# Index pass of a two-layer sparse-attention decoder: head pairs in one rectifier instruction, decode rows two at a time

## The reference

```python
s = jnp.einsum('bqhe,bke->bqhk', qi, ki).astype(jnp.float32)     # 8 index heads of 64
score = jnp.einsum('bqhk,bqh->bqk', jax.nn.relu(s), wi.astype(jnp.float32))
score = jnp.where(admissible[None], score, -jnp.inf)
_, idx = lax.top_k(score, topk)
```

## Time and profile before

| | us |
|---|---|
| median of 3 runs | 5874.4 (5874.07 to 5880.87) |
| profiled execution, its own time | 5873.04 |
| its span | 5871.3 |
| PE busy / PE weight loads | 5420.4 (92%) / 3003.6 |
| DVE busy | 3496.8 (60%) |
| ACT busy | 1748.2 (30%) |
| POOL busy | 1279.0 (22%) |
| mean granted TensorE clock | 0.913 |

### The profile page before, as it was taken

How to read it: one execution, slowest core, us unless ns; L and a number is a source line. 1 busy time by engine, 2 the same in 40 slices (tenths; PEclk the granted TensorE clock), 3 DMA queues, 4 the chain that set the end, 5 groups by cost and what they waited for, 6 DMA issues and landing times.

```text
span 5871.3 us, 75115 instructions
## 1 busy us (share of the span) xinstructions
PE 5420.4 (92%) x25302; PEld 3003.6 (51%) x25302; DVE 3496.8 (60%) x6149; ACT 1748.2 (30%) x3005; POOL 1279.0 (22%) x1215
## 2 busy tenths in 40 slices
PE   7996899999999998999989868999999999889999
PEld 4441344644555556664454314446445556567643
DVE  2561599999877542223425616999997765412234
ACT  2451100100455652220034511001005566522200
POOL 3210034400112871000032100344001128710000
PEclk9895799999999998878998957999999999987899
DMA  1001211211210023544310012112112200245532
GB/s 59 22 4 35 57 36 30 69 48 63 75 58 32 33 67 125 159 146 136 109 36 22 4 37 59 33 31 69 48 62 73 83 9 32 67 127 171 161 97 93
DMA packets 345087, 392.90 MB, mean 67 GB/s; under 512 B 102839, under 2 KB 266770, under 8 KB 341042
## 3 DMA queue, kind: packets, MB, share of 16 engines
q1 hardware_dynamic: 326322, 384.54, 20.9%
q10 hardware_dynamic: 18432, 4.20, 0.3%
HBM read 298.77 MB, written 89.93 MB: 66 GB/s over the span
## 4 chain that ended last, share of the span: by engine, by line
PE 79%; DVE 8%; ACT 4%; issue 4%; ACTq 2%; DMA 1%; POOL 1%; SPq 1%; DVEq 0%; POOLq 0%
PE banks L780 16%; PE banks L783 12%; PE banks L1724 8%; DVE arena L392 4%; PE banks L302 4%; PE banks L1485 4%; PE banks L1053 4%; PE banks L1085 3%; PE banks L1070 3%; PE banks L1510 3%; PE banks L1268 3%; PE banks L1477 2%; PE banks L1283 2%; PE banks L1258 2%; PE banks L541 2%
## 5 line engine op out<-in xcount | busy, mean ns | idle before, releaser
L882 DVE TENSOR_SCALAR_CACHE_REDUCE arena<-arena 128x384 uint8<-128x384 f32 (+14 forms) x960 | 1404.6, 1533 | 6.5
L780 PE MATMUL banks<-arena 128*128 128x512 f32 x2176 | 937.4, 592 | 0.0
L783 PE MATMUL banks<-arena 128*128 128x384 f32 (+3 forms) x2336 | 725.6, 466 | 18.4 <-SPq L146 18.4
L780 PEld LDWEIGHTS banks<-arena 128*128 128x128 f32 x2176 | 409.9, 189 | 523.2 <-issue 523.2
L1313 POOL TENSOR_SCALAR arena<-arena 128x128 f32<-128x128 f32 (+15 forms) x192 | 577.8, 3021 | 144.0 <-DVE arena L1343 144.0
L1169 DVE TENSOR_TENSOR_SCAN arena<-arena 128x129 f32<-128x129 f32 (+3 forms) x480 | 519.3, 1126 | 144.9 <-ACT arena L1097 122.7
L783 PEld LDWEIGHTS banks<-arena 128*128 128x128 f32 (+1 forms) x2336 | 420.1, 184 | 287.5 <-issue 83.2
L1724 PE MATMUL banks<-arena 128*128 128x512 f32 (+1 forms) x1088 | 473.4, 598 | 14.5 <-SPq L146 14.5
L1332 DVE CUSTOM_DVE_ANT_0 arena<-banks,arena 128x512 f32<-128x512 f32 (+3 forms) x480 | 274.1, 608 | 339.0 <-PE banks L1258 318.3
L328 PE MATMUL banks<-arena 64*128 64x512 f32 (+3 forms) x1216 | 423.0, 607 | 22.9 <-ACT arena L374 17.4
L392 DVE SCALAR_TENSOR_TENSOR arena<-arena 128x512 f32<-128x512 f32 (+3 forms) x532 | 401.3, 754 | 55.9 <-DVE arena L392 0.7
(11 more groups left out here) (194 smaller groups left out, 6640.4 us busy)
## 6 DMA issues: line engine op xcount, KB each, us to landing
arena<-in_cache_sb_kv SPq DMA_DIRECT2D x256, 384.0 KB
arena<-in_cache_dsa_kv SPq DMA_DIRECT2D x256, 128.0 KB
arena<-in_x_prompt SPq DMA_DIRECT2D x32, 512.0 KB, 4.4
arena<-mixT SPq DMA_DIRECT2D x32, 512.0 KB, 4.1
arena<-xs SPq DMA_DIRECT2D x32, 512.0 KB, 4.5
arena<-in_w_in SPq DMA_DIRECT2D x8, 1536.0 KB, 7.2
out<-arena SPq DMA_DIRECT2D x64, 192.0 KB, 1.9
mixT<-arena SPq DMA_DIRECT2D x40, 256.0 KB, 2.2
```

Source lines behind the costliest of these rows:

```text
L780: m = nc.tensor.matmul(bank[i % 4][:, :], W2[c % 2][:, k, j * P:(j + 1) * P], xT[:, k, t * FREE:(t + 1) * FREE], start=(k == 0), stop=(k = ...
L783: m = nc.tensor.matmul(bank[i % 4][0:rows_of(t), 0:WD[name]], xT[:, k, t * P:t * P + rows_of(t)], W2[c % 2][:, k, 0:WD[name]], start=(k == ...
L882: nc.vector.tensor_scalar(out[0:r, 0:v.shape[-1]], v, thr[0:r, t:t + 1], 0.0, ALU.is_ge, ALU.add, accum_out=cnt[0:r, t:t + 1]).then_inc(s_ ...
```

## The change

In the index pass a unit is now a pair of heads (t, c, h), h = 0 to 3: two matmuls into two neighbouring banks, one rectifier over both (2 x w columns), two VectorE operations. There are two pair buffers instead of four single ones. The 584 index columns are computed in two halves of 292 for each of the eight slices k, instead of 512 and then 72.

In the decode index pass a unit is a pair of sequences. Their keys stand side by side in 128 columns, so that one transpose serves both; two matmuls on the two halves of the array give 128 rows of products; one matmul with a 128 x 16 `xsel` sums them to 16 rows, which VectorE copies straight to rows 32g to 32g+15 of `scs`. The store to `SCD` and the read back are gone. The hardware loop is written out. VectorE makes two of the five key copies. Three key buffers rotate. The 32 page loads of the first pair are issued by SP in the index pass, at its iteration t = 12; of the other 96, SP issues 64 and ScalarE 32, the latter behind the rectifiers of pairs 0 and 1. `scs` has 128 rows with gaps that are zeroed, so in the stick-breaking stage its store to `SBD` is eight DMAs instead of one. The selection and bias steps work on 128 rows of it instead of 64. `hsel` is made by 16 instead of 8 instructions at the start.

```diff
@@ start_gpsimd
-            v = hsel[:]
-            for h in range(HIDX):
...
+            for e in range(2):
+                v = hsel[:].rearrange("p (q e) -> p q e", e=2)[:, :, e]
+                for h in range(HIDX):
+                    nc.gpsimd.affine_select(out=v, in_=v, compare_op=ALU.not_equal, fill=1.0, base=-e * NS - h * NQ,
...
@@ index pass
-        ir = [carve(FREE) for _ in range(4)]
+        ir = [carve(2 * FREE).rearrange("p (e k) -> p e k", e=2) for _ in range(2)]
...
+                if t == NT - 4:
+                    for e in range(2):
+                        sample_keys_load(sp, l, 0, e)
             for r in range(3):
                 sp.wait_ge(s_ks[r], at(s_ks[r], 16 * (l + 1) * (KSTORES[r] + (KS_EXTRA if r == NT % 3 else 0))))
+            sample_index_queries(sp, l, 0)
...
                     for k in range(KC):
-                        nc.tensor.matmul(bank[0][0:rows_of(s), :], xT[:, k, s * P:s * P + rows_of(s)], W1[:, k, 0:FREE],
-                                         start=(k == 0), stop=(k == KC - 1))
-                    for k in range(KC):
-                        m = nc.tensor.matmul(bank[1][0:rows_of(s), 0:72], xT[:, k, s * P:s * P + rows_of(s)], W1[:, k, FREE:584],
-                                             start=(k == 0), stop=(k == KC - 1))
+                        for v in range(2):
+                            m = nc.tensor.matmul(bank[v][0:rows_of(s), 0:HALFW], xT[:, k, s * P:s * P + rows_of(s)],
+                                                 W1[:, k, v * HALFW:(v + 1) * HALFW], start=(k == 0), stop=(k == KC - 1))
...
-                        for h in range(HIDX):
-                            a = h % 2 * HD
-                            pe.wait_ge(s_ir, at(s_ir, l * NIU + i - 3))
...
+                        for h in range(HIDX // 2):
+                            pe.wait_ge(s_ir, at(s_ir, l * NIU + i - 1))
+                            for e in range(2):
+                                a = e * HD
+                                k = nc.tensor.matmul(bank[4 + 2 * (i % 2) + e][:, 0:w], iqT[t % 2][a:a + HD, h, :], ikT[a:a + HD, c * FREE:c * FREE + w],
+                                                     start=True, stop=True)
+                            k.then_inc(s_iz, 1)
...
-                            act.wait_ge(s_ie, at(s_ie, l * NIU + i - 3))
-                            nc.scalar.activation(ir[b][:, 0:w], bank[4 + b][:, 0:w], ACT.Relu).then_inc(s_ir, 1)
+                            act.wait_ge(s_ie, at(s_ie, 2 * (l * NIU + i - 1)))
+                            nc.scalar.activation(ir[b][:, :, 0:w], z[:, :, 0:w], ACT.Relu).then_inc(s_ir, 1)
...
@@ decode index pass
+        def sample_keys_load(queue, l, g, e):
+            for j in range(NPG):
+                b = 2 * g + e
+                pg = queue.value_load(pages[0:1, b * NPG + j:b * NPG + j + 1], min_val=0, max_val=N_POOL - 1)
+                queue.dma_start(xk[g % 3][:, j, e * HD:(e + 1) * HD], dsa_kidx[l, ds(pg, 1), :, :].rearrange("o p d -> (o p) d")).then_inc(s_xk[g], 16)
...
+            sp.wait_ge(s_xm0, at(s_xm0, 4 * l + 3))
+            new_rows(0)
+            sample_index_queries(sp, l, 1)
+            sample_keys_load(sp, l, 1, 0)
+            sample_keys_load(sp, l, 1, 1)
+            new_rows(1)
+            sample_index_queries(sp, l, 2)
+            sample_keys_load(sp, l, 2, 0)
+            new_rows(2)
...
+            sample_index_queries(sp, l, 3)
+            sample_keys_load(sp, l, 3, 0)
+            new_rows(3)
             load_chunk(sp, l, 0)
...
+            for g in range(NPR):
...
+                pe.wait_ge(s_xk[g], at(s_xk[g], 16 * 34 * (l + 1)))
+                transposes(g, 0)
                 for c in range(NX + 1):
+                    if c + 1 < NX:
+                        transposes(g, c + 1)
                     if c < NX:
...
+                        scores_of(g, c)
+                    if c >= 1:
+                        summed(g, c - 1)
...
+                keys(g, 0)
+                relu(g, 0)
+                keys(g, 2)
+                relu(g, 1)
+                relu(g, 2)
+                keys(g, 4)
+                relu(g, 3)
+                relu(g, 4)
+                if g < 2:
+                    for v in range(2):
+                        act.wait_ge(s_xtf[v], at(s_xtf[v], XU[v] * (n + 1 - g)))
+                    sample_keys_load(act, l, g + 2, 1)
```

More of the change, by code:

```diff
@@ L241, in build @@
         XUSE = (9, 8)
+        HALFW = 292
         KSTORES = [6, 5, 5]
@@ L1014, in stick_sync @@
             sp.wait_ge(s_bias, at(s_bias, l * NSEL + 1))
-            sp.dma_start(SBD[:, :], scs[0:NS, :]).then_inc(s_bs, 16)
+            for b in range(NB):
+                a = 32 * (b // 2) + b % 2
+                sp.dma_start(SBD[b * NQ:(b + 1) * NQ, :], scs[a:a + 2 * NQ - 1:2, :]).then_inc(s_bs, 16)
             load_stick_qk(sp, l, 1)
```

262 lines of the change are left out of this document (117 added, 145 removed).

## The result

The changed kernel takes 5641.8 us in the median of four runs (5636.9 to 5646.1), the kernel before, run in turn with it, 5877.6 us (5874.1 to 5889.2). The ratio is 0.9595, with an interval of 0.9579 to 0.9612: 4.0% faster, where 3.4% was forecast. The profiled execution took 5646.05 us, the slowest of the four; against its sum of 5672.3 that is 26.3 us less, and the terms behind the difference don't all have one sign.

A forecast was written before the change was run, and what follows sets the result against it. The decode index pass was taken as bound by serial copies, issues and half-clock work, not by a full engine. 5873.0 - 217.2 + 4 + 10 + 2.5 = 5672.3 us; forecast's own range 5650 to 5695, 8-in-10 range 5640 to 5715.

The forecast's parts named there:

- What bounds: Decode index pass: no engine fills it; each sequence is a series of copies, eight issues, rectifier, products, sums at half clock.
- The decode index pass: This stage falls to 106 us in each layer, from 212.3 and 216.9, saving 217.2 us in all.
- cheaper issues: Decode index pass: issues cheaper when written out, or pair 2 waits less; 8 us per stage, 5656 us; chance 0.08.
- the rival of half clock throughout: Decode index pass stays at half clock; both stages end at 128 us, total 5716 us; chance 0.13.
- the index pass: Index pass: gain from halves and cost of pairs cancel; +2 for the x tile and +5 for the clock remain per layer.
- The halves: Index pass: columns in 292s instead of 512 and 72 gain 0.77 us per tile at full clock, nothing at half.
- The start of a tile: Index pass: a tile's first DVE operation waits for the whole pair's rectifier, 0.43 us later than before.
- The end of a tile: Index pass: PE's last products start behind a longer rectifier and take longer; next tile's columns start about 0.65 us later.
- the same instructions, at the same pace: Index pass: DVE's scoring with pairs keeps its pace as long as it is fed; no gain or loss booked.
- The clock: Index pass: pairs may thin PE's load and let the clock fall; +5 us per layer, between bounds of zero and 21.
- The x tile: Index pass: 32 page issues at t = 12 delay the load of x tile 13; PE waits, +2 us per layer.
- The read back is gone: End of the decode index pass: the read of the scores from DRAM, for which the next stage waits, disappears.

The follow-up runs named there:

- both_undone: Changed kernel with single heads and columns of 512 and 72 in the index pass again, page loads still at tile 12: 5659.1 us, ratio 0.9602.
- halves_undone: Changed kernel with index columns computed as 512 and 72 again: 5666.1 us, ratio 0.9612.
- pairs_undone: Changed kernel with single heads, four banks and four rectified buffers in the index pass again: 5623.7 us, ratio 0.9557.
- more pages ahead: Changed kernel with first pair's pages at t = 16, second pair's behind them in the index pass, four key buffers: 5599.6 us, ratio 0.9504.
- experiment with the late loads: Changed kernel with the first pair's 32 page loads at t = 16 of the index pass instead of 12: 5629.3 us, ratio 0.956.
- kernel that issues furthest ahead: The kernel with more pages ahead, plus ScalarE issuing 16 page loads of pair 2 between rectifiers of the index pass's last two tiles: 5561.5 us, ratio 0.9456.

## Why the prediction was right or wrong

**What bounds.** Right. The decode index pass was bound by its series of copies, issues and rectifier, and it gave 230.6 us, more than the 226.8 that the span lost.

**The decode index pass.** Right in mechanism, 13.4 us short in size (217.2 booked, 230.6 measured). In layer 0 the stage ended 8.3 us ahead of the forecast: pair 3 began 5.6 us earlier, and from there to the end it took 12.3 us (526.79 to 539.1) where 14 and 1 were booked. Three things make the 5.6. An issue, reckoned as the prediction did, took (34.60 - 0.34) / 31 = 1.11 us on SP and (17.12 - 0.34) / 15 = 1.12, where 1.18 was read off a row of eight; with the register work ahead of each block's first (from the end of the issue before it, at 445.40 for the first block), SP's 64 took 35.9 + 18.4 + 18.4 = 72.7 us and not 75.5. The sum itself was too long by 1.2: it lets SP go on from 45, but 45 has the 1.5 us of pair 1's landing in it, in which SP doesn't wait, so that by its own terms pair 3 was complete at 89.8 and not at 91. The last 1.6 are in the smaller issues and the landing. The rival "cheaper issues", at 8 us a stage, has the right size, with less of it in the issues than it says, and its 5656 is nearer to the profiled run than the forecast; the rival of half clock throughout is out, at 0.70 and 0.72.

**The step that failed is the index pass.** It was booked at +7 us a layer and measured -9.2 and -10.8. The halves, booked at 0.77 a tile or 13.1 a layer, are right: 12.2. Against them stood 20 us: the pairs, 0.43 at the start and 0.65 at the end of each of 12 tiles, 13.0 in all; +5 for the clock; +2 for the x tile. Together these came to 2.2 (12.2 less the 10.0 that the pass lost in the mean). The seams were mis-sized by half, the clock moved the other way there, the x tile cost next to nothing, and DVE's own work got shorter, for which no term stood:

- *The start of a tile*, +0.43 by the longer first rectifier: right. From the next transposes' start, when the columns are done, to DVE's first operation it was 236.31 to 238.81, 2.50 us, and is 261.12 to 264.06, 2.94. It is so at every seam: 2.50 at the first eleven gaps of the kernel before and of both versions with single heads, 2.94 at those of the kernel after. The timeline of the kernel before, and of the one after:

```profile
236.31 0.60 PE L315 MATMUL banks<-ident,arena 128*128 128x128 f32 x4
```

```profile
261.12 0.60 PE L319 MATMUL banks<-ident,arena 128*128 128x128 f32 x4
...
262.93 1.94 ACT L381 ACTIVATE arena<-banks 128x1024 f32<-128x1024 f32 x2 [0.19 <-PE banks L333]
...
264.06 0.77 DVE L396 TENSOR_SCALAR arena<-arena 128x512 f32<-128x512 f32 x1 [10.38 <-ACT arena L381]
```

- *The end of a tile*, +0.65: too dear. It was priced at a last chunk of 512, where the rectifier is 0.43 longer; but a tile's last chunk ends on the diagonal and is narrower in three tiles of four. At the seam after tile 9, where PE takes up the transposes of tile 13, it is 256 wide, and the pair's rectifier takes 0.60 us (row below) where two single ones had 0.38 each. PE took up these transposes 2.71 us before DVE ended (254.80 against 253.49 + 4.02 = 257.51), and now 2.53 before (251.15 against 253.68): 0.18 dearer.

```profile
247.67 0.60 ACT L381 ACTIVATE arena<-banks 128x512 f32<-128x512 f32 x1 [0.69 <-DVE arena L399]
...
249.66 4.02 DVE L399 SCALAR_TENSOR_TENSOR arena<-arena 128x256 f32<-128x256 f32 x7
```

```profile
253.49 4.02 DVE L392 SCALAR_TENSOR_TENSOR arena<-arena 128x256 f32<-128x256 f32 x7
```

  The same lead of PE over DVE's end at the other seams (layer 0, us, after tiles 2 to 12; behind tile 13 no x tile is left to transpose):

```
before  5.25 5.44 2.33 2.70 3.18 4.59 2.24 2.71 3.91 4.59 2.86
after   5.45 5.89 2.21 2.49 2.85 4.16 2.13 2.53 3.58 4.16 2.53
```

  A last chunk of 512 (tiles 7, 11) costs 0.43, one of 384 (6, 10) 0.33, one of 256 (5, 9) 0.2, one of 128 0.1 (4, 8) or 0.3 (12); after tiles 2 and 3 PE is earlier with pairs, by 0.20 and 0.45. With 0.44 for each start the twelve seams come to some 7 us a layer, 0.6 each, where 13.0 was booked. The gaps, under each the time that the granted clock stood at half from 2.7 us ahead of the gap to its end, show the rest (layer 0, us, after tiles 2 to 13):

```
both_undone     6.8 6.6 12.1 11.6 10.9 7.5 11.8 11.7 8.1 7.5 11.5 9.0
 at half        0.0 0.0  5.3  4.7  3.7 0.0  4.5  4.7 0.0 0.0  5.1 2.7
halves_undone   7.0 6.6 12.4 11.9  8.9 9.6 11.7 11.9 8.9 8.3 12.8 9.7
 at half        0.0 0.0  4.8  4.1  0.0 0.2  3.4  4.1 0.0 0.0  6.3 2.7
pairs_undone    6.1 5.9 11.1 11.2 10.6 6.7 10.3 11.4 7.4 6.7  9.9 9.0
 at half        0.0 0.0  4.8  5.2  4.6 0.0  3.0  4.7 0.0 0.0  3.4 2.5
after           6.3 5.9 11.0 11.2  9.1 7.6 12.4 10.4 8.2 7.6 10.7 9.7
 at half        0.0 0.0  3.6  4.2  0.2 0.0  6.3  2.5 0.0 0.0  3.4 2.8
```

  Where neither of the last two versions met half clock, after tiles 2, 3, 7, 10 and 11, the gap grew by 0.2, 0.0, 0.9, 0.8 and 0.9 us, which is the start and the end of that seam. At the others the clock blurs the price, by up to 2 us either way, and on the whole it pays some of it back: the 12 gaps have less time at half clock with pairs in all four comparisons, 23.0 us for 28.1 in the table's last two, 25.8 for 30.8 in its first two, 22.8 for 27.3 and 26.6 for 32.7 in layer 1. An instruction of 292 columns took 487 ns from start to start at half clock and 248 at full; if half of such time is lost, which is an estimate from these figures, the clock gives 2.3 to 3.1 us a layer back. Seams of 7 less that are 3.9 to 4.7, and the gaps of layer 0 grew by 3.7 to 4.8; in layer 1 they grew by 4.8 and 1.8, the second of which this sum doesn't reach. What lets the clock fall at a seam of one version and not at the same one of another isn't settled.

- *DVE's stretches* are 1.7 or 1.8 us a layer shorter with pairs, in three comparisons of either layer (with the halves, without, and with more pages ahead). This was forecast as "the same instructions, at the same pace". The group on 512 columns went from 839 to 818 ns. At the start of tile 9's scoring the seven operations behind the first take 6.96 us in the kernel after and 7.33 in the one before (rows below); they begin later against POOL's six rotary steps, which run only then. Sorted by what POOL does meanwhile, the group falls apart: in layer 0 of the kernel before, 47 of its 196 operations lie beside a rotary step or POOL's copy and take 1.10 to 1.12 us each, and the 136 beside nothing 0.75; in the kernel after it is 36 and 147, at the same two prices. Eleven fewer at 0.36 are 3.9 us. The first operation of a tile, also beside POOL, takes 0.75 instead of 0.53 in the mean, 2.6 us more over 12 tiles. That accounts for 1.3 of the 1.8. No run moves POOL's steps by themselves.

```profile
235.94 6.96 DVE L399 SCALAR_TENSOR_TENSOR arena<-arena 128x512 f32<-128x512 f32 x7
```

```profile
239.40 7.33 DVE L392 SCALAR_TENSOR_TENSOR arena<-arena 128x512 f32<-128x512 f32 x7
```

- *The clock*, +5 a layer: nothing over the whole pass. The windows have 0.94 and 0.93, before 0.94 and 0.92, and at the seams it gave something back, as above. PE was busy for 333 of the 421 us instead of 398 of 430, and late in the pass it waits in every pair, yet the stretch from 396 to 436, of the kind that held 1.00, held 0.96:

```profile
396.00:436.00 40.00, 29.01 (x102) 8.30 (x104) 35.31 (x53) 25.47 (x27) 0.40 (x1) 0.96 0.01 2
```

Some tiles still begin at half clock (251.15, with 1.97 us for eight transposes, as in the earlier trace rows): 7 of the 12 gaps met it, as in the version without pairs or halves. The Trainium skill's rule ("TensorE: Matmul & The Clock Gate", "Part 1: The HAM clock gate (the 'warmup' mystery)"), under which only a whole idle window lets the clock fall, gave nothing for this term, and nothing came. It still doesn't account for the half clock of the earlier trace rows in the kernel before, where PE was counted busy for all of the 2.00 us.

- *The x tile*, +2: next to nothing, 0.5 and 0.2 with both edits undone. As the rows above show, SP was there 4.3 us earlier and each issue 0.07 cheaper than booked. The experiment with the late loads found nothing to gain.

**What was not in the sum.** The projections' stage lost 3.0 and 2.3 us. Before, PE came out of a pause of 9.37 us (the read back of the earlier trace rows) and took 8.71 us for its first 17 matmuls; now it waits 1.48 and does 30 in 9.93, 0.33 each instead of 0.51:

```profile
659.70 8.71 PE L783 MATMUL banks<-arena 128*128 128x384 f32 x17 [9.37 <-SPq L146]
```

```profile
539.27 9.93 PE L804 MATMUL banks<-arena 128*128 128x384 f32 x30 [1.48 <-POOLq L147]
```

17 times 0.18 is 3.1. The granted clock was 0.50 from 659.7 to 665.7 before, and it is 1.00 over the 9.93 us now. The step "the read back is gone" counted the wait and not the cold start behind it.

**The start**, +2.5: 3.2 measured, of which the mask instructions, now 16 in 5.24 us instead of 8 in 2.48, are 2.8.

**The decode attention.** The changed kernel's profiled run spent 25.9 us more there, with unchanged code. Most of the eight sequences of a layer take one of two times, some 51 us or 58 to 61; the first takes 63 to 66, and a few take 55. In the kernel before, three of layer 1:

```profile
5233.50:5284.40 50.90, 46.78 (x276) 31.66 (x275) 13.50 (x43) 12.95 (x26) 0.00 (x0) 0.90 0.56 175
5335.60:5394.80 59.20, 55.43 (x277) 41.19 (x276) 13.48 (x43) 13.16 (x26) 0.00 (x0) 0.77 0.48 150
5394.80:5455.40 60.60, 56.97 (x277) 42.78 (x276) 13.49 (x43) 13.23 (x26) 0.00 (x0) 0.75 0.47 147
```

in the kernel after, one of the long kind:

```profile
5041.00:5102.00 61.00, 57.17 (x278) 43.01 (x276) 13.49 (x43) 13.16 (x26) 0.00 (x0) 0.75 0.46 146
```

The work is the same (276 matmuls), the granted clock is 0.90 in the short kind and 0.75 to 0.77 in the long. Before, layer 1 had four short ones among the seven after its first; after it had one, the last. Over the twelve profiled runs the stage takes 451 to 487 us, in both directions, the kernel before by itself 7 us between two runs. The changed kernel's second profiled run spent 17.9 us more than the kernel before there, so 8 of the 25.9 are of the one execution. Whether the rest is chance or the changed kernel's own isn't settled: with this decode index pass, but other edits ahead of the same stage code, both layers together took 909.9 to 971.3 us, against 915.3 and 922.3 in the two runs of the kernel before. No term of the prediction holds these 25.9, and they are why the sum of -34.0 for the index pass, -13.4 for the decode index pass, -5.3 for the projections, +0.7 for the start, +25.9 and -0.2 elsewhere is only -26.3. Without them the run would lie 52 us under the forecast, so part of the forecast's nearness is luck. What flips a sequence from one kind to the other stays open.

**Which part of the change does it.** The decode pass by pairs, its pages ahead, gives 4.0% (both undone: 0.9602), the halves 24 us of index pass, and the pairs take 3 to 6 us back, in both layers together. In whole times the pairs can't be told from nothing, and the halves barely: 0.9612 [0.9588, 0.9636] without them, 0.9565 [0.9541, 0.959] with them.

## What to carry to other kernels

When a stage is a queue of DMA issues, count the issues and multiply: here 1.07 to 1.11 us each on SP and 1.03 on ACT by a row's length over its count (from issue to issue 1.11 to 1.13 and 1.06 to 1.08), with the 16 DMA engines 0.21 busy, and every issue moved out of the stage was worth its full price until the queue no longer ended last, 97.7, 81.1, 63.7. An edit's price at the seam of two tiles is to be read from the shape that stands at the seam, not from the most frequent one: here it ran from 0.0 to 0.9 us by the tile. And before the total is explained, compare the stages whose code didn't change: 25.9 us of the difference lay in one of them.

## What the runs showed of the hardware

The page loads' cost is the issue, on the engine that issues. The Trainium skill ("DMA: Bandwidth & Descriptors", "Issuing engines are not separate DMA queues") says that issuing from several engines saves only sequencer time, which it calls usually small beside the DMA itself. The runs agree with the first half, and not with the second for these loads: with 0.21 of the DMA engines' time used, 32 issues fewer in the stage's SP queue were worth 37.1 and 34.4 us.

A single page issued between two rectifiers shows 0.36 us on ACT's queue, in the kernel that issues furthest ahead, and a block of 16 takes 1.03 each; what lies between two issues is in a group's row and not in that of a lone one:

```profile
392.78 0.36 ACTq L477 DMA_DIRECT2D arena<-in_cache_dsa_kidx  x1
```

So the 0.34 of a last issue is no measure of such a load.
